# A residual seeded into the PSUM accumulators of a mixture-of-experts layer by identity products, with the final norm read from PSUM

## Chip, cores and metric

The kernel runs on one core of a Trainium2 chip. The metric is the device time of one execution in microseconds (us). Three executions of the kernel before took 1356.05, 1356.93 and 1356.97 us, median 1356.93. The profile and the trace come from a further execution of the same program.

Names used below: PE is TensorE (PEld its weight loads), DVE is VectorE, ACT is ScalarE, POOL is GpSimd, SP is SyncE, which issues most transfers.

## What is computed

One layer on 256 tokens of 1024 channels, all in float32: a mixer (causal pooling and a gated DeltaNet), then a top-4-of-32 mixture of experts, each with its residual, then a final RMSNorm. The part that matters here, cut from the reference:

```python
h = rmsnorm(x, norm_ffn_g[l]) * (1.0 + sc2) + sh2
x = x + gt2 * moe_ffn(h, router_w[l], router_b[l], exp_w1[l], exp_b1[l], exp_w2[l], exp_b2[l])
...
return rmsnorm(x, final_norm_g)

def rmsnorm(x, g):
    y = xf * lax.rsqrt(jnp.mean(xf * xf, axis=-1, keepdims=True) + RMS_EPS)
    return (y * g.astype(jnp.float32)).astype(x.dtype)
```

`moe_ffn` adds up, for each token, four experts' outputs with their gate weights, and each expert's bias `b2` with the same weight.

## The kernel before

The program is written by hand: each engine has its own list of instructions, in the order in which they stand, and the engines meet by semaphores. Nothing reorders the work.

**Weights.** All large weights pass through `ring`, six slots of 2 MB in SBUF. SP waits until a slot is free (`used[s]`, raised by the last product that reads it) and issues the next chunk into it (L504 in `stream`). An expert is six chunks: slots 0 to 3 hold w1, slots 4 and 5 the two halves of w2. SP issues them strictly in this order, so a slot that is late holds back those behind it. The chunks of expert 0 are loaded ahead; those of expert 1 onward wait for the routing (`vec_route`) and for block 0 to free the slots.

**Blocks.** The tokens of an expert are served in blocks of 64 (`SLOTS`). Blocks run in order of experts; here one expert has two blocks and each other one, 33 in all. Block 0 is written out, `serve` is the loop's body, `serve_last` the last block. For a block n PE does: `bias` (L1330), the w1 products (`hidden`, L1338), the gather of the next block's tokens (L1309), `combine` of block n - 1 (L1384), and `finish_block`: transposes (L1402, L1322, L1316) and the w2 products (L1372), which free slots 4 and 5 at their ends. In block 0, where there is no earlier block to combine, `biases_out` (L1396) stands in its place.

**Accumulators.** The layer's output for the 2 x 128 tokens and 2 x 512 channels is held in four PSUM banks, 4 to 7, over the whole expert loop. `biases_out` starts them with the gated b2 biases (`start=True`); each `combine` adds a block to them (`start=False`). The halves h = 0 and h = 1 of such a pair of products stand on different partitions of their operands (0 and 64), and so on different row groups of the array.

**Tail.** The last `combine` raises `pe_moe` after each half of the tokens. DVE adds the residual `xt` to each bank (`add_experts`, L1902) into `fin`; ACT squares the sums and accumulates the row sums (`fin_square`, L775); DVE turns one of each pair of sums into a half mean (L1906), ACT takes the root (L784), DVE its reciprocal (L1911), then scales by it and by the final gain (L1914). SP writes out each quarter (L520).

`ident` is a 128 x 128 identity matrix. `xt` lies in the tile `region_x` and has held the residual stream since the mixer's end; `fin` lies in `qkv`, `b2_rows` in `work`, `gatewT` in `region_z`.

Of the kernel before, what the change touches and what calls it, by code (L numbers as in the profile page):

```python
# [20 lines left out]
ALU = mybir.AluOpType  # L21
ACT = mybir.ActivationFunctionType
# [90 lines left out]
def program(nc, x, c, ada_w, ada_b, norm_mix_g, norm_ffn_g, w_in, conv_w, pool_w, pool_scale, a_log,  # L113
            dt_bias, gdn_norm_g, w_pool_out, w_gdn_out, w_out, router_w, router_b, exp_w1, exp_b1,
            exp_w2, exp_b2, final_norm_g, const, out):
    with ExitStack() as ctx:
        ctx.enter_context(nc.allow_non_contiguous_dma(reason="small parameter rows"))

        def sb(name, shape, dt=F32):
            return ctx.enter_context(nc.sbuf_tensor(name, shape, dt))  # L120

        def sem(name):
            return ctx.enter_context(nc.semaphore(name))
# [22 lines left out]
        small = sb("small", [P, 48])  # L146
        blocks_i = sb("blocks_i", [1, 2 * P + E + 1], I32)

        def const_tile(name):
            o, w = CONST[name]  # L150
            return consts[:, o:o + w]

        ident = const_tile("ident")
# [8 lines left out]
        xt = region_x[:, :].rearrange("p (t d) -> p t d", t=T)  # L162
# [51 lines left out]
        def take(n, parts=P):  # L214
            nonlocal m
            a = work[0:parts, m:m + n]
            m += n
            return a
# [17 lines left out]
        fin_g = take(D)  # L236
        fin = q_of.rearrange("p h s -> p (h s)").rearrange("p (t d) -> p t d", t=T)
        fin_sq = xn2
# [15 lines left out]
        bank = [ctx.enter_context(nc.psum_tensor(f"bank{i}", [P, 512], F32)) for i in range(8)]  # L254
# [18 lines left out]
        fin_in = sem("fin_in")  # L273
# [123 lines left out]
        pe_moe = sem("pe_moe")  # L397
# [8 lines left out]
        vec_b2 = sem("vec_b2")  # L406
        vec_blocks = sem("vec_blocks")
        act_fin = sem("act_fin")
        vec_fin = sem("vec_fin")
        vec_rms = sem("vec_rms")  # L410
        act_rms = sem("act_rms")
        vec_out = sem("vec_out")
# [24 lines left out]
        for n, (kind, _) in enumerate(chunks):  # L437
            chunk_no.setdefault(kind, []).append(n)
# [130 lines left out]
        def _(act):  # L569
# [201 lines left out]
            nc.scalar.activation(stat[:, 1, 2:3], small[:, 16:17], ACT.Sqrt)  # L771

            def fin_square(i):
                act.wait_ge(vec_fin, i + 1)
                nc.scalar.activation(fin_sq[:, i // 2, (i % 2) * 512:(i % 2 + 1) * 512],  # L775
                                     fin[:, i // 2, (i % 2) * 512:(i % 2 + 1) * 512], ACT.Square,
                                     accum_out=stat[:, 0, i:i + 1]).then_inc(act_fin, 1)

            for t in range(T):
                fin_square(2 * t)  # L780
                fin_square(2 * t + 1)
                act.wait_ge(act_fin, 2 * t + 2)
                act.wait_ge(vec_rms, t + 1)
                nc.scalar.activation(small[:, 20 + t:21 + t], stat[:, 0, 2 * t + 1:2 * t + 2], ACT.Sqrt, scale=1.0 / D,  # L784
                                     bias=small[:, 18 + t:19 + t]).then_inc(act_rms, 1)
# [3 lines left out]
        def _(pe):  # L789
# [141 lines left out]
            for r in range(2):  # L931
                for j in range(4):
# [3 lines left out]
                                          start=(r == 0), stop=(r == 1))  # L936
# [40 lines left out]
            for r in range(4):  # L977
                pe.wait_ge(pool_sq, 2 * r + 2)
                for j in range(4):
                    mm = nc.tensor.matmul(bank[4][32 * j:32 * j + 32, 0:S], pick[:, 31 - r:63 - r],  # L980
                                          sq[:, 2 * r + j // 2, (j % 2) * S:(j % 2 + 1) * S],
                                          start=(r == 0), stop=(r == 3))
# [17 lines left out]
            for r in range(4):  # L1000
                if r:
                    pe.wait_ge(vec_norm, 4 * r)
                for j in range(4):
# [3 lines left out]
                                          start=True, stop=True)  # L1007
# [47 lines left out]
            for g in range(2):  # L1055
                hs = [HG * g + h for h in range(HG)]
                lo, hi = slice(0, HALF), slice(HALF, P)
                for t in range(T):
# [8 lines left out]
                    for h in hs:  # L1067
                        nc.tensor.matmul(quad(3 * t + 1)[:, h % HG], k_of[:, h, tok], k_of[:, h, tok],
                                         start=True, stop=True)
                    for h in hs:  # L1070
                        mm = nc.tensor.matmul(quad(3 * t + 2)[:, h % HG], k_of[:, h, tok], q_of[:, h, tok],
                                              start=True, stop=True)
# [26 lines left out]
                else:  # L1099
                    for k in range(KC):  # L1100
                        mm = nc.tensor.matmul(bank[6][:, 0:E], mod[:, 24 + k:25 + k].to_broadcast([P, P]), rw[:, k, :],
                                              start=(k == 0), stop=(k == KC - 1))
                    mm.then_inc(pe_spread, 1)

                def turn_l(t):
                    for h in range(HG):
# [5 lines left out]
                                 start=True, stop=True).then_inc(pe_oct, 1)  # L1112
# [21 lines left out]
                for i, s in enumerate(LEVELS):  # L1134
                    z_tile(2 * g + 1, 1, 2 * i, 2 * i + 2)
                    for t in range(T):
                        pe.wait_ge(pool_off, 10 * g + 2 + 2 * i + (t + 1 if i else 2 - t))
                        pe.wait_ge(vec_inv, 10 * g + 2 * i + t + 1)
                        for h in range(HG):
                            if s < HALF:  # L1140
                                mm = nc.tensor.matmul(quad(3 * t + 1)[:, h], off[:, t, h], inv[:, t, h],  # L1141
                                                      start=True, stop=True)
                            else:
                                mm = nc.tensor.matmul(quad(3 * t + 1)[hi, h, lo], off[lo, t, h, hi], inv[lo, t, h, lo],
                                                      start=True, stop=True)
                        mm.then_inc(pe_prod, 1)
                    for t in range(T):
# [3 lines left out]
                        if s < HALF:  # L1151
# [4 lines left out]
                            for h in range(HG):  # L1156
                                mm = nc.tensor.matmul(quad(3 * t + 2)[:, h], prod[:, t, h], invT[:, t, h],  # L1157
                                                      start=True, stop=True)
                        else:
                            for h in range(HG):  # L1160
                                mm = nc.tensor.matmul(quad(3 * t + 2)[lo, h, hi], prod[hi, t, h, lo], invT[hi, t, h, hi],
                                                      start=True, stop=True)
                        mm.then_inc(pe_corr, 1)
                for t in range(T):
# [3 lines left out]
                    if t:  # L1168
                        for h in range(HG):
                            mm = nc.tensor.matmul(quad(3 * t + 1)[:, h], kbg[:, t, h], invT[:, t, h],  # L1170
                                                  start=True, stop=True)
# [17 lines left out]
                for h in range(HG):  # L1189
                    mm = nc.tensor.matmul(quad(3)[:, h], q_of[:, HG * g + h, P:2 * P], state[:, h],  # L1190
                                          start=True, stop=True)
# [100 lines left out]
            for t in range(T):  # L1292
                mm = nc.tensor.matmul(bank[5][:, t * E:(t + 1) * E], const_tile("before"), mask[:, t, :],
                                      start=True, stop=(t == 0))
# [94 lines left out]
            def biases_out():  # L1389

                pe.wait_ge(vec_route, 1)
                pe.wait_ge(vec_b2, 2)
                for t in range(T):
                    for h in range(2):
                        at = slice(h * SLOTS, h * SLOTS + E)
                        nc.tensor.matmul(bank[4 + 2 * t + h][:, :], gatewT[at, t * P:(t + 1) * P], b2_rows[at, :],  # L1396
                                         start=True, stop=False, skip_group_check=True)

            def turn_sel(n):
                pe.wait_ge(vec_wsel, n + 1)  # L1400
# [23 lines left out]
            def serve_last(n):  # L1424
# [21 lines left out]
                             start=True, stop=True).then_inc(pe_route, 1)  # L1446
# [15 lines left out]
            w1_chunk(0, 3)  # L1462
            gather(1)
            biases_out()
            finish_block(0)
            n_last = further_blocks(pe, serve)
# [5 lines left out]
        def _(dve):  # L1472
            chain = [0]

            def link(*steps):

                for ins in steps:
                    chain[0] += 1
                    ins.then_inc(vec_chain, 1)
                dve.wait_ge(vec_chain, chain[0])  # L1480

            tt, ts, stt = nc.vector.tensor_tensor, nc.vector.tensor_scalar, nc.vector.scalar_tensor_tensor
# [413 lines left out]
            serve(0)  # L1896
            serve(further_blocks(dve, serve), last=True)

            def add_experts(t, half):
                cut_ = slice(half * 512, (half + 1) * 512)  # L1900
                dve.wait_ge(pe_moe, t + 1)
                tt(fin[:, t, cut_], bank[4 + 2 * t + half][:, :], xt[:, t, cut_], ALU.add).then_inc(vec_fin, 1)  # L1902

            def half_of_squares(t):
                dve.wait_ge(act_fin, 2 * t + 1)
                ts(small[:, 18 + t:19 + t], stat[:, 0, 2 * t:2 * t + 1], 1.0 / D, EPS, ALU.mult, ALU.add)\  # L1906
                    .then_inc(vec_rms, 1)

            def scale_out(t):
                dve.wait_ge(act_rms, t + 1)  # L1910
                link(recip(small[:, 22 + t:23 + t], small[:, 20 + t:21 + t]))  # L1911
                for half in range(2):
                    cut_ = slice(half * 512, (half + 1) * 512)
                    stt(fin[:, t, cut_], fin[:, t, cut_], small[:, 22 + t:23 + t], fin_g[:, cut_],  # L1914
                        ALU.mult, ALU.mult).then_inc(vec_out, 1)

            add_experts(0, 0)
            add_experts(0, 1)
            half_of_squares(0)
            add_experts(1, 0)  # L1920
            add_experts(1, 1)
            half_of_squares(1)
            dve.wait_ge(fin_in, 16)
            scale_out(0)
            scale_out(1)


# [25 lines left out]
```

## Time and profile before

| | |
|---|---|
| median of three executions | 1356.93 us (1356.05 to 1356.97) |
| the profiled execution's own time | 1355.68 us |
| its span in the trace | 1353.3 us |
| PE busy | 1282.3 us, 95% |
| DVE, ACT, POOL busy | 391.3, 188.2, 48.3 us |
| mean TensorE clock granted | 0.997 of full speed |
| moved by DMA | 471.71 MB, mean 349 GB/s |

Busy shares are means over stages with different limits. The stages here are the mixer (up to about 390 us), block 0 of the experts, the expert loop, and a tail of some 10 us after the last product. In the loop the share of the DMA engines and that of PE are both close to full, so the waits have to be read, not the shares.

### The profile page before, as it was taken

How to read it: one execution, taken by the hardware profiler on the slowest of the kernel's cores; microseconds unless marked ns; L12 is line 12 of the kernel's file. 1: busy time of each engine (PE TensorE's matmuls, PEld its weight loads, DVE VectorE, ACT ScalarE, POOL GpSimd, SP SyncE). 2: the span in 40 equal slices, each digit the busy share in tenths (PEclk: the TensorE clock that was granted, in tenths of full speed). 3: DMA queues.
4: the chain of work that ended last, by engine and by line, in shares of the span. 5: the costliest groups of instructions: out<-in, count | busy, mean ns of one | idle time of the engine just before them, and what ended most of it. 6: DMA issues, size and time to landing. Idle time of an engine off the chain costs nothing.

```text
span 1353.3 us, 17457 instructions
## 1 busy us (share of the span) xinstructions
PE 1282.3 (95%) x6549; PEld 624.1 (46%) x6550; DVE 391.3 (29%) x982; ACT 188.2 (14%) x401; POOL 48.3 (4%) x48
## 2 busy tenths in 40 slices
PE   7999999999999999989999998999999999999997
PEld 5788878898653333223333322333333322333332
DVE  1599574732252211112111111211211111121112
ACT  1110223422120110001100000100010000011001
POOL 1020012220000000000000000000000000000000
PEclk9999999999999999999999999999999999999999
DMA  9998550008349999999999999699999999999996
GB/s 334 357 375 299 206 187 1 1 27 316 124 152 407 426 426 426 425 426 426 428 426 426 426 425 426 253 427 423 426 429 426 426 427 425 426 425 429 427 426 248
DMA packets 69079, 471.71 MB, mean 349 GB/s; under 512 B 4093, under 2 KB 4410, under 8 KB 36154
## 3 DMA queue, kind: packets, MB, share of 16 engines
q1 hardware_dynamic: 68224, 469.62, 84.5%
q10 hardware_dynamic: 538, 1.13, 0.3%
q0 software_dynamic: 288, 0.55, 0.2%
q8 instruction: 21, 0.34, 0.1%
q14 instruction: 8, 0.07, 0.0%
HBM read 470.23 MB, written 1.05 MB: 348 GB/s over the span
## 4 chain that ended last, share of the span: by engine, by line
PE 54%; DMA 42%; DVE 1%; SPq 1%; ACT 1%; issue 1%; DVEq 0%
DMA ring<-in_exp_w_dram 40%; PE bank L1338 18%; PE bank L806 12%; PE bank L1372 6%; PE bank L1235 2%; DMA ring<-in_ada_w_dram 2%; PE bank L1024 2%; PE bank L1384 2%; PE bank L1309 2%; PE bank L900 1%; PE bank L1330 1%; PE bank L1157 1%; PE bank L1141 1%; PE bank L1154 1%; SPq L487 1%
## 5 line engine op out<-in xcount | busy, mean ns | idle before, releaser
L1338 PE MATMUL bank<-ring,work 128*64 128x512 f32 x2112 | 470.6, 596 | 47.3 <-DMA ring<-in_exp_w_dram 47.3
L1338 PEld LDWEIGHTS bank<-ring,work 128*64 128x64 f32 x2112 | 144.6, 137 | 368.9 <-issue 272.2
L1372 PE MATMUL bank<-ring,work 128*64 128x512 f32 x1056 | 234.1, 595 | 0.9 <-ACT work L749 0.5
L1372 PEld LDWEIGHTS bank<-ring,work 128*64 128x64 f32 x1056 | 72.9, 137 | 137.9 <-issue 136.6
L756 ACT ACTIVATE work<-work 128x256 f32<-128x256 f32 x66 | 27.5, 416 | 765.1 <-DVE work L1863 765.1
L1863 DVE TENSOR_SCALAR work<-bank 128x256 f32<-128x256 f32 x66 | 27.6, 419 | 350.4 <-PE bank L1338 350.4
L806 PE MATMUL bank<-region_h,ring 128*128 128x256 f32 x576 | 126.6, 380 | 0.0
L806 PEld LDWEIGHTS bank<-region_h,ring 128*128 128x128 f32 x576 | 108.8, 190 | 14.4
L1893 DVE TENSOR_TENSOR work<-bank,work 128x512 f32<-128x512 f32 x33 | 22.8, 692 | 313.8 <-PE bank L1372 313.8
L1384 PE MATMUL bank<-work 64*128 64x512 f32 x264 | 65.6, 615 | 0.8 <-DVE work L1893 0.8
L1309 PE MATMUL bank<-qkv,work 128*64 128x512 f32 x264 | 62.3, 592 | 0.2 <-DVE work L1801 0.2
L1879 DVE TENSOR_SCALAR work<-consts,region_z 128x128 f32 (+1 forms) x66 | 19.9, 345 | 87.7 <-issue 87.7
L1870 DVE TENSOR_TENSOR work<-work 128x256 f32<-128x256 f32 x66 | 40.7, 617 | 12.3 <-DVE work L1866 12.3
L1384 PEld LDWEIGHTS bank<-work 64*128 64x128 f32 x264 | 22.7, 186 | 43.2 <-issue 41.5
L1309 PEld LDWEIGHTS bank<-qkv,work 128*64 128x64 f32 x264 | 19.0, 137 | 37.4 <-issue 37.4
L1330 PE MATMUL bank<-work 32*64 32x512 f32 x264 | 35.9, 612 | 0.3 <-issue 0.3
L1505 DVE SCALAR_TENSOR_TENSOR region_z<-ring,c_act,region_z 128x512 f32<-128x512 f32 x48 | 35.6, 809 | 0.0
L1538 DVE SCALAR_TENSOR_TENSOR qkv<-bank,conv_cols,qkv 128x255 f32<-128x255 f32 (+2 forms) x72 | 31.3, 477 | 1.3
L900 PE MATMUL bank<-region_h,ring 128*128 128x256 f32 x128 | 28.8, 382 | 1.3 <-DVE region_h L1523 1.3
L1024 PE MATMUL bank<-region_h,ring 128*128 128x256 f32 x128 | 29.6, 379 | 0.0
L806 PE MATMUL bank<-region_z,ring 128*128 128x256 f32 x128 | 27.9, 380 | 1.0 <-DVE region_z L1736 1.0
L1866 DVE SCALAR_TENSOR_TENSOR work<-work 128x256 f32<-128x256 f32 x66 | 28.0, 425 | 2.3
(304 smaller groups left out, 953.6 us busy)
## 6 DMA issues: line engine op xcount, KB each, us to landing
ring<-in_exp_w_dram SPq DMA_DIRECT2D x190, 2048.0 KB, 23.6
ring<-in_ada_w_dram SPq DMA_DIRECT2D x12, 2048.0 KB, 12.4
ring<-in_w_in_dram SPq DMA_DIRECT2D x11, 2048.0 KB, 12.8
ring<-in_w_in_dram SPq DMA_DIRECT2D x4, 1024.0 KB, 17.2
ring<-in_w_gdn_out_dram SPq DMA_DIRECT2D x2, 2048.0 KB, 11.7
ring<-in_w_out_dram SPq DMA_DIRECT2D x2, 2048.0 KB, 16.6
ring<-in_exp_w_dram SPq DMA_DIRECT2D x4, 1024.0 KB, 23.5
ring<-in_w_pool_out_dram SPq DMA_DIRECT2D x1, 2048.0 KB, 8.4
```

The lines of the kernel that those rows point to most:

```text
L806: mm = nc.tensor.matmul(out_ap, w(k) if w else w_slot(n, j, k), rhs[:, k, :], start=(k == 0), stop=(k == kc - 1))
L900: mm = nc.tensor.matmul(pair(i)[:, a, :], w_slot(n, 2 * (i % 2) + a, k), hT[:, k, :], start=(k + a == 0), stop=(k == KC - 1), skip_group_c ...
L1024: mm = nc.tensor.matmul(pair(7)[:, a, :], w_slot(n, j, k), hT[:, k, :], start=(k == 0), stop=(k == KC - 1))
L1309: mm = nc.tensor.matmul(bank[3][h * SLOTS:(h + 1) * SLOTS, :], sel[:, t, :], h2[:, t, h * 512:(h + 1) * 512], start=(t == 0), stop=(t == T ...
L1330: nc.tensor.matmul(bank[b][h * SLOTS:(h + 1) * SLOTS, :], onehot[b * SLOTS:b * SLOTS + E, :], b1_rows[b * SLOTS:b * SLOTS + E, h * 512:(h ...
L1338: mm = nc.tensor.matmul(bank[b][h * SLOTS:(h + 1) * SLOTS, :], xT[:, c % 4, c // 4, :], slot_as(q, 2)[:, i, lo:lo + 512], start=False, sto ...
L1372: mm = nc.tensor.matmul(bank[2][o * SLOTS:(o + 1) * SLOTS, :], actT[:, b, c, h, :], slot_as(4 + b, 2)[:, h, lo:lo + 512], start=(b + h + c ...
L1384: mm = nc.tensor.matmul(bank[4 + 2 * t + h][:, :], wselT[at, t * P:(t + 1) * P], y_nat[at, :], start=False, stop=last, skip_group_check=True)
L1505: ins = stt(half, w[:, k, :], c_act[:, k:k + 1], half, ALU.mult, ALU.add)
L1538: steps.append(stt(qkv[:, f, shift:S], src[:, a, 0:S - shift], w, qkv[:, f, shift:S], ALU.mult, ALU.add))
L1866: stt(lin[:, b, :], lin[:, b, :], 1.0, glu[:, b, :], ALU.add, ALU.mult).then_inc(vec_lin, 1)
L1870: tt(act_nat[:, b, :].rearrange("q (c p) -> q p c", c=2), lin[:, b, :].rearrange("q (p c) -> q p c", c=2), sig[:, b, :].rearrange("q (p c) ...
```

## The change

Each of the four accumulators is now started by an identity product of the residual (`ident` times `xt`, K = 128, 512 columns), and the bias product is added to it. `add_experts` and its semaphore `vec_fin` go. ACT's squares wait for the last `combine` and read the PSUM banks; DVE's scaling reads the banks too and writes `fin`. The scaling is split in single quarters, with the second half mean between the first two and the wait for the final gain (`fin_in`) ahead of the first reciprocal.

```diff
@@ scalar engine, fin_square
-                act.wait_ge(vec_fin, i + 1)
-                nc.scalar.activation(fin_sq[:, i // 2, (i % 2) * 512:(i % 2 + 1) * 512],
-                                     fin[:, i // 2, (i % 2) * 512:(i % 2 + 1) * 512], ACT.Square,
+                act.wait_ge(pe_moe, i // 2 + 1)
+                nc.scalar.activation(fin_sq[:, i // 2, (i % 2) * 512:(i % 2 + 1) * 512], bank[4 + i][:, :], ACT.Square,
                                      accum_out=stat[:, 0, i:i + 1]).then_inc(act_fin, 1)
@@ tensor engine, biases_out
+                        nc.tensor.matmul(bank[4 + 2 * t + h][:, :], ident, xt[:, t, h * 512:(h + 1) * 512],
+                                         start=True, stop=False, skip_group_check=True)
                         nc.tensor.matmul(bank[4 + 2 * t + h][:, :], gatewT[at, t * P:(t + 1) * P], b2_rows[at, :],
-                                         start=True, stop=False, skip_group_check=True)
+                                         start=False, stop=False, skip_group_check=True)
@@ vector engine, tail
-            def add_experts(t, half):
-                cut_ = slice(half * 512, (half + 1) * 512)
-                dve.wait_ge(pe_moe, t + 1)
-                tt(fin[:, t, cut_], bank[4 + 2 * t + half][:, :], xt[:, t, cut_], ALU.add).then_inc(vec_fin, 1)
...
-            def scale_out(t):
+            def invert(t):
                 dve.wait_ge(act_rms, t + 1)
                 link(recip(small[:, 22 + t:23 + t], small[:, 20 + t:21 + t]))
-                for half in range(2):
-                    cut_ = slice(half * 512, (half + 1) * 512)
-                    stt(fin[:, t, cut_], fin[:, t, cut_], small[:, 22 + t:23 + t], fin_g[:, cut_],
-                        ALU.mult, ALU.mult).then_inc(vec_out, 1)
-
-            add_experts(0, 0)
-            add_experts(0, 1)
+
+            def scale_out(t, half):
+                cut_ = slice(half * 512, (half + 1) * 512)
+                stt(fin[:, t, cut_], bank[4 + 2 * t + half][:, :], small[:, 22 + t:23 + t], fin_g[:, cut_],
+                    ALU.mult, ALU.mult).then_inc(vec_out, 1)
+
             half_of_squares(0)
-            add_experts(1, 0)
-            add_experts(1, 1)
+            dve.wait_ge(fin_in, 16)
+            invert(0)
+            scale_out(0, 0)
             half_of_squares(1)
-            dve.wait_ge(fin_in, 16)
-            scale_out(0)
-            scale_out(1)
+            scale_out(0, 1)
+            invert(1)
+            scale_out(1, 0)
+            scale_out(1, 1)
```

PE's order in block 0, from the gather for block 1 to the transposes of `finish_block`, before (`bankN` are PSUM banks; `work` and `region_z` hold `b2_rows` and `gatewT`):

```order
L1309 MATMUL bank3<-qkv,work 64x512 x4
L1396 MATMUL bank4<-work,region_z 128x512
L1396 MATMUL bank5<-work,region_z 128x512
L1396 MATMUL bank6<-work,region_z 128x512
L1396 MATMUL bank7<-work,region_z 128x512
L1402 MATMUL bank2<-consts,work 128x128 x2
```

And with the change (the lines above it move up by two, so L1307 is the gather that was L1309; `consts` holds `ident`, `region_x` holds `xt`):

```order
L1307 MATMUL bank3<-qkv,work 64x512 x4
L1394 MATMUL bank4<-region_x,consts 128x512
L1396 MATMUL bank4<-work,region_z 128x512
L1394 MATMUL bank5<-region_x,consts 128x512
L1396 MATMUL bank5<-work,region_z 128x512
L1394 MATMUL bank6<-region_x,consts 128x512
L1396 MATMUL bank6<-work,region_z 128x512
L1394 MATMUL bank7<-region_x,consts 128x512
L1396 MATMUL bank7<-work,region_z 128x512
L1402 MATMUL bank2<-consts,work 128x128 x2
```

An identity product now stands ahead of each bias product; the four bias products no longer follow one another.

DVE's order from the last block's scaling by `gt2` to its end, before:

```order
L1893 TENSOR_TENSOR work<-bank2,work 128x512
L1902 TENSOR_TENSOR qkv<-bank4,region_x 128x512
L1902 TENSOR_TENSOR qkv<-bank5,region_x 128x512
L1906 TENSOR_SCALAR small<-stat 128x1
L1902 TENSOR_TENSOR qkv<-bank6,region_x 128x512
L1902 TENSOR_TENSOR qkv<-bank7,region_x 128x512
L1906 TENSOR_SCALAR small<-stat 128x1
L1911 RECIPROCAL small<-small 128x1
L1914 SCALAR_TENSOR_TENSOR qkv<-qkv,small,work 128x512 x2
L1911 RECIPROCAL small<-small 128x1
L1914 SCALAR_TENSOR_TENSOR qkv<-qkv,small,work 128x512 x2
```

And with the change:

```order
L1893 TENSOR_TENSOR work<-bank2,work 128x512
L1901 TENSOR_SCALAR small<-stat 128x1
L1906 RECIPROCAL small<-small 128x1
L1910 SCALAR_TENSOR_TENSOR qkv<-bank4,small,work 128x512
L1901 TENSOR_SCALAR small<-stat 128x1
L1910 SCALAR_TENSOR_TENSOR qkv<-bank5,small,work 128x512
L1906 RECIPROCAL small<-small 128x1
L1910 SCALAR_TENSOR_TENSOR qkv<-bank6,small,work 128x512
L1910 SCALAR_TENSOR_TENSOR qkv<-bank7,small,work 128x512
```

The four adds are gone, the scalings read the banks, and the second half mean stands between the first two scalings instead of ahead of all four.

## Rows read from the trace of the kernel before

**Rows 1.** The page: PE's busy time, and GB/s in 40 slices of the span.
```profile
PE 1282.3 (95%) x6549; PEld 624.1 (46%) x6550; DVE 391.3 (29%) x982; ACT 188.2 (14%) x401; POOL 48.3 (4%) x48
...
GB/s 334 357 375 299 206 187 1 1 27 316 124 152 407 426 426 426 425 426 426 428 426 426 426 425 426 253 427 423 426 429 426 426 427 425 426 425 429 427 426 248
```

**Rows 2.** The chain that ended last, 420 to 500 us: start, length, what.
```profile
454.80 13.88 PE bank L1338 x64
...
481.60 13.88 PE bank L1338 x64
```

**Rows 3.** The same chain, 1000 to 1100 us.
```profile
1062.27 3.68 PE bank L1338 x16
...
1091.79 3.68 PE bank L1338 x16
```

**Rows 4.** The same chain, 800 to 960 us.
```profile
817.15 25.64 DMA ring<-in_exp_w_dram
...
842.83 3.65 PE bank L1338 x16
```

**Rows 5.** Windows: length, each engine's busy us, clock, DMA share, GB/s.
```profile
400.00:405.00 5.00, 5.00 (x28) 1.52 (x26) 1.46 (x9) 0.34 (x1) 0.00 (x0) 1.00 0.00 0
...
540.00:545.00 5.00, 4.46 (x24) 1.29 (x22) 0.00 (x0) 0.00 (x0) 0.00 (x0) 1.00 0.99 419
```

**Rows 6.** Two single issues into the ring, SP, tile view: duration ns, start, landing.
```profile
L504 SPq DMA_DIRECT2D ring<-in_exp_w_dram x1: 384/384/384, 423.7 to 423.7; - x1
...
DMA to landing us min/median/max: 10.8/10.8/10.8
...
L504 SPq DMA_DIRECT2D ring<-in_exp_w_dram x1: 342/342/342, 863.2 to 863.2; - x1
...
DMA to landing us min/median/max: 7.3/7.3/7.3
```

**Rows 7.** The chain that ended last, 380 to 560 us.
```profile
382.88 3.53 PE bank L1235 x8
...
415.09 1.72 PE bank L1309 x8
416.81 1.92 PE bank L1396 x8
418.73 0.37 PE bank L1402 x2
419.10 0.22 PE bank L1322 x2
```

**Rows 8.** Weight loads of L1235: duration ns min/median/max, first and last start.
```profile
L1235 PEld LDWEIGHTS bank<-ring,region_y x64: 188/190/192, 355.6 to 385.4; 128*128 128x128 f32 x64
```

**Rows 9.** Timeline of the tail: start, us, engine, line, what [idle before <- releaser].
```profile
1342.68 0.69 DVE L1893 TENSOR_TENSOR work<-bank,work 128x512 f32<-128x512 f32 x1 [7.69 <-PE bank L1372]
...
1344.61 1.29 DVE L1902 TENSOR_TENSOR qkv<-bank,region_x 128x512 f32<-128x512 f32 x2 [1.23 <-PE bank L1384]
1345.33 0.63 ACT L775 ACTIVATE qkv<-qkv 128x512 f32<-128x512 f32 x1 [4.89 <-DVE qkv L1902]
...
1346.70 0.29 ACT L784 ACTIVATE small<-stat,small 128x1 f32<-128x1 f32 x1
...
1347.63 0.15 DVE L1906 TENSOR_SCALAR small<-stat 128x1 f32<-128x1 f32 x1 [0.20 <-ACT qkv L775]
1347.71 0.16 DVE L1911 RECIPROCAL small<-small 128x1 f32<-128x1 f32 x1
1347.91 1.42 DVE L1914 SCALAR_TENSOR_TENSOR qkv<-qkv,small,work 128x512 f32<-128x512 f32 x2
...
1348.25 0.29 ACT L784 ACTIVATE small<-stat,small 128x1 f32<-128x1 f32 x1
...
1349.43 1.41 DVE L1914 SCALAR_TENSOR_TENSOR qkv<-qkv,small,work 128x512 f32<-128x512 f32 x2
```

**Rows 10.** A copy from PSUM by ACT, timeline of the routing.
```profile
397.10 0.60 ACT L741 ACTIVATE work<-bank 128x512 f32<-128x512 f32 x1 [3.59 <-PE bank L1309]
```

More of the change, by code:

```diff
@@ L408, in program @@
         act_fin = sem("act_fin")
-        vec_fin = sem("vec_fin")
         vec_rms = sem("vec_rms")
```

## The prediction

> **What bounds the kernel now.** I read the page first, then the chain of waits, then the weight transfers one by one, then the last 12 us. On the page TensorE is busy 95% of the span, yet the GB/s row stands at about 426 in nearly every slice from the twelfth on [rows 1]: two resources run close to each other, and which one sets the pace has to be read stretch by stretch. In the chain, early in the expert loop, nothing but TensorE appears and one expert takes 481.60 - 454.80 = 26.8 us [rows 2]. Later the same line starts again after each landing of a weight transfer, 1091.79 - 1062.27 = 29.5 us apart [rows 3]. Six chunks of 2 MB are an expert, so a chunk takes 29.5 / 6 = 4.92 us of DMA. TensorE needs 2.7 us less per expert than the DMA engines do; a lead or a lag of TensorE is used up, a lag of the transfers is kept. The one expert that has two blocks does not free it: TensorE waits for a landing at 842.79 just before it [rows 4], and the transfers that restart in its second block are set off by TensorE's own progress, so they inherit any lag.
>
> So what counts of the first block is when its slots are freed. The DMA engines are idle at 400 to 405 us [rows 5]: all six slots are full and the routing is being worked out. The stream starts at 406, fed by slots as block 0 frees them. The fifth chunk of the second expert is issued at 423.7, when the first half of the w2 product has ended, and lands 10.8 us later, at 434.5. A chunk that is issued to idle DMA engines lands after 7.3 us (the issue at 863.2) [rows 6]. The fifth chunk therefore has 10.8 - 7.3 = **3.5 us of slack**; past that, each microsecond TensorE loses before it frees this slot moves the whole stream.
>
> **Part 1: four identity products in the first block.** They stand between gather(1) and finish_block(0), ahead of both w2 products, so ahead of the release of the fifth slot. TensorE works without a gap there (the chain has only TensorE across that stretch), so all they add is added in full.
> - Identity product: K = 128, 128 columns of weights, 512 moving columns, float32. The same form is L1235: eight records, two for each product, in 3.53 us [rows 7], 0.88 us each. Four: 3.5 us.
> - The four bias products take 1.92 us today [rows 7] because the two halves stand on different row groups (partitions 0 and 64) and run side by side, two at a time: 4 steps, (1.92 - 0.2) / 4 = 0.43 us each. With a full-array product between any two of them they can't pair. Alone each takes its two passes, 0.86 us. Four: 3.4 us.
> - Change of array shape: eight of them where there was one. The four steps of L1396 take 1.92 us, eight steps of L1309 without a change take 1.72, so going into a row group costs 0.2 us; L1402's two transposes after it take 0.37, L1322's two 0.22, so going back costs 0.15 [rows 7]. Four each way: 1.4 us. Bounds: 0 us, if the next weight load hides under the running product; and 0.35 us each, 2.8 us, if a whole weight load (0.19 us [rows 8]) and the 0.15 both show. I take 1.4, since the rows nearest are the very changes in question.
>
> Together 3.5 + 3.4 + 1.4 = 8.3 us, say 8.4, in place of 1.92: TensorE is **6.5 us later** at finish_block(0) (bounds 5.0 and 7.8). The Trainium skill, page "TensorEngine Tiling (Array Packing)", section "Tiling Modes", says that changing the tiling mode drains TensorE, while changing only the tile doesn't. By that rule the 1.4 us belong in the sum; without a drain the sum below would be 1.4 us smaller, at +0.3. The trace agrees so far, with 0.15 to 0.2 us at the two changes.
>
> Slip of the stream: 6.5 - 3.5 = **3.0 us** (bounds 1.5 and 4.3). The chunks behind have more slack: the sixth is freed 3.5 us after the fifth (half of the w2 work), less than a chunk's 4.92, and TensorE gains 2.7 us per expert. The rest of TensorE's lag, 3.5 us, is gone within two experts, so its first wait for a landing comes one or two experts later than now (between 540 and 545 us [rows 5]). At the end only the 3.0 us stay. The Trainium skill, page "DMA: Bandwidth & Descriptors", section "Anatomy of one DMA", gives 2.0 us fixed plus bytes at 436 GB/s: as an estimate 6.8 us for a 2 MB chunk, so 4.0 us of slack and a sum 0.5 us lower. The trace has 7.3, and it decides.
>
> **Part 2: the tail.** Today VectorE adds the residual (two 512-column adds, 0.64 us apart), and only then ScalarE squares. Now ScalarE starts when TensorE has ended half 0 of the combine.
> - The first square moves from 1345.33 to 1344.61 [rows 9], 0.72 us earlier. ScalarE's row of work is as before: a 512-column read of PSUM takes 0.60 us [rows 10], the square from SBUF some 0.61. Its roots move from 1346.70 to 1345.98 and from 1348.25 to 1347.53, ending 1347.82.
> - VectorE loses four adds. It is no longer held by the second pair and the half mean behind it (1347.63) before it can scale. Reciprocal at 1346.31, first scaling 0.20 later (as 1347.71 to 1347.91) at 1346.51; 0.71 each. It reads PSUM now; L1893 does that in 0.69. Then the half mean (0.08), second scaling to 1348.01, reciprocal (0.10), two more scalings to 1349.53. Today they end at 1349.43 + 1.41 = 1350.84. **Gain 1.3 us.** The bound is now VectorE's four scalings; ScalarE's second root is in time by 0.2 us. The four output transfers keep following the scalings; the last one's 2 us to landing stay.
> - The dropped semaphore and the earlier wait for the final gain vector cost nothing: that vector is loaded ahead of the expert loop.
> - Bounds: 0 if the new reads of PSUM stretch ScalarE's row by 0.3 us per square; 1.4 if scalings take 0.69.
>
> **Sum.** 3.0 - 1.3 = **+1.7 us**. Against the profiled execution's own time of 1355.68 us this gives 1357.4. That execution lies 1.25 us below the median of the runs, 1356.93, so for a median I say 1358.6. A measurement of this kernel tells about 0.2% from no change, 2.7 us, so I forecast no difference that can be told.
>
> **Rivals.**
> 1. *The stream doesn't slip (12%).* If the products overlap better than the rows say, or the fifth chunk's transfer has other slack, the first block's loss is hidden and only the tail counts: -1.3 us, 1355.6. For: transfers bound the loop and TensorE has 2.7 us per expert to spare. Against: the slack is 3.5 us by two rows, and even without any cost of changing shape TensorE is 5.0 us late.
> 2. *Slower than can be overlooked (12%).* Every change between full array and row group shows a full weight load as well as a drain, 0.35 us. Then TensorE is 7.8 us late, the stream slips 4.3, the sum is +3.0: 1359.9. It decides from a lag of 7.5 us on, that is when the eight products take over 9.4 us, 1.18 us each. Against: the two changes of shape in the rows show 0.15 and 0.2 only; for: those stand behind a pair or behind short transposes, not behind a 512-column product.
> 3. *The tail gives nothing (6%).* ScalarE or VectorE reads of PSUM run slower while TensorE still writes the other two accumulators. Then +3.0 us, 1359.9, slower. Against: L1893 and the 0.60 us copies read PSUM beside a busy TensorE at full rate.
> 4. *Faster by over 0.2% (2%).* It would need more than the tail holds: the whole tail after the last combine is under 10 us and 1.3 of it go.
>
> **How the numbers follow.** Forecast 68%: a sum between +0.2 and +2.6, likeliest +1.7. With rival 1 inside the 0.2% as well, same is 0.80; rivals 2 and 3 give slower 0.17; faster 0.03. The range goes from rival 1 to rival 2, 1355.6 to 1359.9, with 0.2 and 0.7 us for the 0.9 us by which the three runs differ: 1355.4 to 1360.6.
>
> **What would show it.** In the trace of the changed kernel: L1394 and L1396 together 8.2 to 8.6 us from first start to the transposes of L1402, eight products without overlap; the fifth chunk of the second expert issued near 430.2 and landing near 437.5, with DMA engines idle for 2 to 3 us between 428 and 431; TensorE's first wait for a landing one or two experts later; the landing that now comes at 842.79 near 845.8; the first square right behind the first half of the last combine and the last scaling some 5.0 us after that square begins (now 6.2 from the first add). Wrong: a chunk that lands at 434.5 as before, or a block 0 longer by over 7.5 us.

## The result and the profile after

| | before | with the change |
|---|---|---|
| median, us | 1356.55 (1355.12 to 1359.87, 20 runs) | 1359.61 (1357.81 to 1361.64, 20 runs) |
| ratio | | 1.002, 95% interval 1.0013 to 1.0026 |
| profiled execution: span, us | 1353.3 | 1357.6 |

The change costs 3.1 us, some 0.2%: at the border of what I had called no difference, though the interval leaves out 1. The median lies in the range I gave (1355.4 to 1360.6), 1.0 us above the value I gave. Against the median of the kernel before, the likeliest sum was +1.7, and 3.1 were measured.

Not all 4.3 us between the two spans belong to the change. The mixer ahead of it, which it doesn't touch, varies from execution to execution: the first chunk that block 0 sets off is issued at 406.1 in the trace of before, at 407.4 here, and between 405.4 and 410.0 in all traces below. So I measure from that issue on. From it to the end of the span it is 1353.3 - 406.1 = 947.2 us before and 1357.6 - 407.4 = 950.2 with the change: **+3.0 us**, which is what the medians say.

The chain of waits in block 0 of the changed kernel, the answer to L1309, L1396 and L1402 in [rows 7] (start, length, what):

```profile
416.36 1.72 PE bank L1307 x8
418.07 1.06 PE bank L1394 x2
419.13 1.05 PE bank L1396 x2
420.18 1.05 PE bank L1394 x2
421.24 1.05 PE bank L1396 x2
...
424.39 1.06 PE bank L1394 x2
425.45 1.05 PE bank L1396 x2
426.50 0.37 PE bank L1402 x2
```

Eight products, each alone, 1.05 us each. From 418.07 to 426.50 it is 8.43 us where 1.92 stood: TensorE is 6.5 us late, as forecast. The full-array products (128 rows) take 1.05 us here, while L1235, the same form, takes 0.88 in a row of its like: the change of shape adds to the product instead of hiding under it.

What the DMA engines did meanwhile (windows of 5 us; the last column is GB/s):

```profile
425.00:430.00 5.00, 5.00 (x26) 2.27 (x26) 0.00 (x0) 1.53 (x4) 0.00 (x0) 1.00 0.72 306
430.00:435.00 5.00, 5.00 (x28) 1.51 (x28) 0.19 (x1) 0.00 (x0) 0.00 (x0) 1.00 0.52 136
```

In place of a steady 426 GB/s there is a hole: by the packets in the trace fewer than half of the 16 DMA engines work from 428.7 us on, and none between 430.1 and 432.5. The fifth chunk of the second expert is the next issue, the answer to the first of [rows 6]:

```profile
L503 SPq DMA_DIRECT2D ring<-in_exp_w_dram x1: 384/384/384, 431.5 to 431.5; - x1
...
DMA to landing us min/median/max: 7.6/7.6/7.6
```

It lands 7.6 us after its issue, as a chunk does that finds nothing ahead of it; before it took 10.8. Counted from the first issue it lands at 431.5 + 7.6 - 407.4 = 31.7 us, before at 28.4: the stream slips 3.3 us here.

The tail, the answer to [rows 9]:

```profile
1349.00 1.99 PE L1382 MATMUL bank<-work 64*128 64x512 f32 x8 [0.79 <-DVE work L1893]
1350.18 0.60 ACT L774 ACTIVATE qkv<-bank 128x512 f32<-128x512 f32 x1 [4.16 <-PE bank L1382]
...
1351.48 0.29 ACT L782 ACTIVATE small<-stat,small 128x1 f32<-128x1 f32 x1
...
1351.87 0.17 DVE L1906 RECIPROCAL small<-small 128x1 f32<-128x1 f32 x1 [0.82 <-ACT small L782]
1352.07 0.75 DVE L1910 SCALAR_TENSOR_TENSOR qkv<-bank,small,work 128x512 f32<-128x512 f32 x1
...
1352.80 0.74 DVE L1910 SCALAR_TENSOR_TENSOR qkv<-bank,small,work 128x512 f32<-128x512 f32 x1
...
1353.65 1.41 DVE L1910 SCALAR_TENSOR_TENSOR qkv<-bank,small,work 128x512 f32<-128x512 f32 x2
```

ScalarE starts 1.18 us after the combine's start, where VectorE's add stood before, and the last scaling ends 1355.06 - 1350.18 = 4.88 us behind that; it was 1350.84 - 1344.61 = 6.23. The tail gives the 1.3 us of the sum.

So the trace holds 3.3 of loss, 1.3 of gain and +3.0 in all. One more microsecond is lost somewhere after the fifth chunk. It is in a single landing. It is the tenth chunk of the stream, five behind the late one. Issue and time to landing of the ninth and the tenth, first in the changed kernel:

```profile
L503 SPq DMA_DIRECT2D ring<-in_exp_w_dram x1: 333/333/333, 446.4 to 446.4; - x1
...
DMA to landing us min/median/max: 12.4/12.4/12.4
...
L503 SPq DMA_DIRECT2D ring<-in_exp_w_dram x1: 333/333/333, 449.8 to 449.8; - x1
...
DMA to landing us min/median/max: 14.9/14.9/14.9
```

They land at 458.8 and 464.8, 6.0 us apart (the figures shown are rounded; here and in the table below I take intervals from unrounded times). The same two chunks in the kernel before:

```profile
L504 SPq DMA_DIRECT2D ring<-in_exp_w_dram x1: 333/333/333, 438.6 to 438.6; - x1
...
DMA to landing us min/median/max: 15.5/15.5/15.5
...
L504 SPq DMA_DIRECT2D ring<-in_exp_w_dram x1: 332/332/332, 442.1 to 442.1; - x1
...
DMA to landing us min/median/max: 17.0/17.0/17.0
```

454.1 and 459.0, 4.9 apart. In the changed kernel the DMA queues show something else there (the window of 458 to 460 us; packets, MB, share of 16 engines' time):

```profile
q1 hardware_dynamic: 66, 0.88, 105.3%
q8 instruction: 1, 0.02, 3.3%
```

One packet of the queue that loads instructions: 3.3% of 16 engines' 2 us is 1.06 us of one engine. The kernel before has one too, at 450 to 452 us, with no widened interval around it. Whether the step (so I call such a widened interval) belongs to the change was the open question.

### The profile page after: what moved, and what is told of

Same layout as the page of the kernel before. It is cut to its first block, busy times and chain, and to the rows that moved or that the text cites. A ratio compares the mean times of both kernels' runs of the same rounds, so it can differ in the third digit from the quotient of the medians.

```text
span 1357.6 us, 17469 instructions
## 1 busy us (share of the span) xinstructions
PE 1291.4 (95%) x6557; PEld 628.0 (46%) x6558; DVE 388.5 (29%) x978; ACT 188.1 (14%) x401; POOL 48.3 (4%) x48
## 3 DMA queue, kind: packets, MB, share of 16 engines
HBM read 470.23 MB, written 1.05 MB: 347 GB/s over the span
## 4 chain that ended last, share of the span: by engine, by line
PE 56%; DMA 40%; DVE 1%; SPq 1%; ACT 1%; issue 1%; DVEq 0%
DMA ring<-in_exp_w_dram 38%; PE bank L1336 19%; PE bank L804 12%; PE bank L1370 7%; PE bank L1233 2%; DMA ring<-in_ada_w_dram 2%; PE bank L1022 2%; PE bank L1382 2%; PE bank L1307 2%; PE bank L898 1%; PE bank L1328 1%; PE bank L1155 1%; PE bank L1139 1%; PE bank L1152 1%; SPq L486 1%
## 5 line engine op out<-in xcount | busy, mean ns | idle before, releaser
L1863 DVE TENSOR_SCALAR work<-bank 128x256 f32<-128x256 f32 x66 | 27.6, 418 | 348.2 <-PE bank L1336 348.2
L1307 PE MATMUL bank<-qkv,work 128*64 128x512 f32 x264 | 62.3, 592 | 0.2 <-DVE work L1801 0.2
L1307 PEld LDWEIGHTS bank<-qkv,work 128*64 128x64 f32 x264 | 19.0, 137 | 37.5 <-issue 37.5
L804 PE MATMUL bank<-region_z,ring 128*128 128x256 f32 x128 | 27.9, 380 | 1.0 <-DVE region_z L1736 1.0
```

The costliest lines, as they stand in the source:

```text
L804: mm = nc.tensor.matmul(out_ap, w(k) if w else w_slot(n, j, k), rhs[:, k, :], start=(k == 0), stop=(k == kc - 1))
L1307: mm = nc.tensor.matmul(bank[3][h * SLOTS:(h + 1) * SLOTS, :], sel[:, t, :], h2[:, t, h * 512:(h + 1) * 512], start=(t == 0), stop=(t == T ...
```

## The experiments

Three theories. **A**, that of the prediction: the stream slips by TensorE's lag less 3.5 us, and nothing else happens. **B**: a stream that ran dry loses more than that. **C**: the tail gives less in the time than in the trace. After the first four, B was made more exact as **D**: the extra loss is one step of about 1 us at a packet of the instruction queue, and only where the stream has run dry before (its mechanism stands in what was expected of 14 spare products).

For each kernel the table gives TensorE's lag when block 0 frees the fifth slot (for the two late kernels, then when it frees the next slot, that of the first chunk of the third expert), the landing of the fifth chunk of the second expert from the first issue, the interval that stands out behind it, the time from the first issue to TensorE's restart ahead of the expert with two blocks (842.83 - 406.1 = 436.7 before), and from the first issue to the end of the span. All are differences of starts, landings and spans in the traces, good to 0.1 us.

| kernel | lag | fifth lands | step later | to the restart | to the end | time against before (measured together) |
|---|---|---|---|---|---|---|
| before | 0 | 28.4 | none | 436.7 | 947.2 | |
| before, again | 0 | 28.2 | none | 436.5 | 946.9 | |
| the change | 6.5 | 31.7 | 6.0 | 441.1 | 950.2 | 1.002 (1.0013 to 1.0026) |
| the change, again | 6.5 | 31.6 | 6.0 | 441.1 | 950.1 | |
| identity products, old tail | 6.5 | 31.6 | 6.2 | 441.3 | 951.7 | 1.0029 (1.0018 to 1.0040) |
| new tail alone | 0 | 28.3 | none | 436.7 | 946.1 | 0.9987 (0.9978 to 0.9996) |
| grouped | 3.6 | 28.7 | 6.1 | 438.2 | 947.3 | 1.0001 (0.9992 to 1.0010) |
| grouped, late | -1.6, then 4.0 | 28.4 | none | 436.9 | 946.0 | 0.9984 (0.9975 to 0.9993) |
| alternating, late | -1.6, then 6.8 | 28.3 | 6.1 | 439.5 | 948.7 | 1.0001 (0.9992 to 1.0010) |
| 8 spare products | 1.8 | 28.3 | none | 436.8 | 947.2 | |
| 14 spare products | 3.2 | 30.8 | none | 439.2 | 949.6 | 1.0011 (1.0001 to 1.0020) |
| 14 spare, again | 3.2 | 31.0 | none | 439.4 | 950.2 | |
| 30 spare products | 6.7 | 31.9 | 6.0 | 441.2 | 951.9 | 1.0036 (1.0023 to 1.0049) |
| 60 spare products | 13.4 | 38.6 | 6.5 | 448.4 | 958.9 | 1.0086 (1.0073 to 1.0099) |

An interval without a step is 4.9 to 5.0 us (4.75 once, right behind the step of 6.5).

**Identity products with the old tail.** To `biases_out` of the kernel before:

```diff
+                        nc.tensor.matmul(bank[4 + 2 * t + h][:, :], ident, xt[:, t, h * 512:(h + 1) * 512],
+                                         start=True, stop=False, skip_group_check=True)
                         nc.tensor.matmul(bank[4 + 2 * t + h][:, :], gatewT[at, t * P:(t + 1) * P], b2_rows[at, :],
-                                         start=True, stop=False, skip_group_check=True)
+                                         start=False, stop=False, skip_group_check=True)
```

Expected: 

> The kernel before with the four identity products added in the first block and its old tail (so the residual is counted twice in the output). Theory A (the stream slips by TensorE's lag less 3.5 us of slack, nothing else): block 0 is 6.5 us longer, the transfers from the fifth chunk of the second expert on 3.0 us late, +3.0 us in time. Theory B (running dry costs the stream something beyond the slip): +4.0 to +4.6 us. If both were wrong and the loop hid the products: 0.

Measured: median 1360.58 against 1357.02, +3.6; in the trace +4.5 from the first issue to the end, of it 4.6 ahead of the restart. This is B's number in the trace; the times alone (+2.4 to +5.4) would leave A's +3.0 open. It is also the first half of the sum by itself: 3.3 at the fifth chunk and the step again.

**The new tail alone.** The changed kernel with

```diff
-                        nc.tensor.matmul(bank[4 + 2 * t + h][:, :], ident, xt[:, t, h * 512:(h + 1) * 512],
-                                         start=True, stop=False, skip_group_check=True)
                         nc.tensor.matmul(bank[4 + 2 * t + h][:, :], gatewT[at, t * P:(t + 1) * P], b2_rows[at, :],
-                                         start=False, stop=False, skip_group_check=True)
+                                         start=True, stop=False, skip_group_check=True)
```

Expected: 

> The changed kernel without the four identity products (the output lacks the residual of the experts' half). Theory A and B: first block and stream as before, the last scaling ends 1.3 us earlier behind the last combine, -1.3 us. Theory C (the tail's gain is smaller in the time than in the trace, which would explain that the change cost 3.1 and not 1.7): 0 to -0.3 us.

Measured: 1354.76 against 1357.02, ratio 0.9987, -1.8 us with an interval of -3.0 to -0.5; in the trace -1.1. The tail's gain is real and C falls: its 0 to -0.3 lies outside.

**Grouped.** The four identity products first, then the bias products in pairs:

```diff
                 for t in range(T):
                     for h in range(2):
-                        at = slice(h * SLOTS, h * SLOTS + E)
                         nc.tensor.matmul(bank[4 + 2 * t + h][:, :], ident, xt[:, t, h * 512:(h + 1) * 512],
                                          start=True, stop=False, skip_group_check=True)
+                for t in range(T):
+                    for h in range(2):
+                        at = slice(h * SLOTS, h * SLOTS + E)
                         nc.tensor.matmul(bank[4 + 2 * t + h][:, :], gatewT[at, t * P:(t + 1) * P], b2_rows[at, :],
                                          start=False, stop=False, skip_group_check=True)
```

Expected: 

> The changed kernel with the four identity products first and the four bias products behind them, in pairs again. Theory A: identity 3.5 us, biases 1.9, two changes of array shape in place of eight: block 0 is 3.7 us longer, the stream slips 0.2 us, the tail gives 1.3: -1.1 us against before. Theory B: the stream runs dry for a moment all the same, +0 to +0.5 us. If the pairing did not come back (products to one bank, one behind the other): about as the change, +1.7.

The chain of its block 0:

```profile
416.54 3.63 PE bank L1393 x8
420.17 1.92 PE bank L1398 x8
422.08 0.37 PE bank L1404 x2
```

The pairs are back: 5.55 us for the same eight products that take 8.43 in turns. The order of four lines is worth 2.9 us of TensorE's time. The fifth chunk lands 0.3 us late, A's number. Then comes a step to 6.1 us, and the kernel is no faster than before (median 1356.54 against 1357.02, ratio 1.0001): B's number.

**Grouped and late.** The same, and

```diff
-            biases_out()
             finish_block(0)
+            biases_out()
```

Expected: 

> As the grouped one, with all eight products behind the w2 products of block 0 instead of ahead of them. The fifth and sixth slot are then freed 1.9 us earlier than before; the next slot (first chunk of the third expert) is freed 3.7 us later than before and has 12.6 - 7.3 = 5.3 us of slack. Theories A and B: no slip, only the tail, -1.3 us. If TensorE's lag itself counted and not the slots: as the grouped one placed ahead.

Measured: 1354.56 against 1357.02, ratio 0.9984 with an interval of 0.9975 to 0.9993, to the end 946.0 against 947.2. The DMA engines never stop, there is no step, and the tail's gain is left whole. This is the version that beats both kernels: 2.5 us below before in the medians of the runs taken together, and 5.0 below the median of the change, which was timed in other runs. It does the same work on TensorE as the grouped one; only which slots wait for it differs. The slots of w2 are freed 1.6 us earlier than before, the next one 4.0 later.

**Spare products: the price of a lag by itself.** The kernel before with 14, 60, 30 and 8 products of the identity by itself, 0.22 us each, into a bank that is free there:

```diff
             biases_out()
+            keep_warm(14, 2)
             finish_block(0)
```

Expected of 14: 

> The kernel before with 14 spare 128x128 products of the identity (0.22 us each, 3.1 us) ahead of finish_block(0), nothing else. Theory A (slip = lag less 3.5 us): no slip, 0. Theory D (each of the 16 DMA engines has its own backlog; a fetch of instructions of 16 KB holds one of them back by about 1 us; a second fetch costs nothing as long as an earlier one has left another engine further behind, and costs in full once a dry moment has let that one catch up): the dry moment has only just begun at 3.1 us, slip 0 to 0.9 us.

Expected of 60: 

> As the kernel with 14 spare products, with 60 of them: 13.2 us. Theory A: slip 9.7 us, and +9.7 in time. Theory D: 9.7 at once at the fifth chunk of the second expert, and 1.0 to 1.3 more in one single later chunk, where the trace has the next packet of the instruction queue: +10.8. Theory B as I first put it (a dry stream costs in proportion): more than 12.

Expected of 30: 

> As the kernel with 14 spare products, with 30 of them: 6.6 us, the lag of the change without its identity products and without any change of array shape between products. Theory A: slip 3.1 us. Theory D: 3.1 us at the fifth chunk and 1.0 to 1.3 in one later one, +4.2. If the new products did something beyond taking TensorE's time (a slower read of an operand, a bank), this one would stay at less than the kernel with the identity products and the old tail (slip 4.5 us).

Expected of 8: 

> Eight spare products, 1.8 us, half of the slack. Theory A and D: the fifth chunk lands 28.4 us after the first issue as before, and the loop is as before, 436.7 us from the first issue to the wait ahead of the expert with two blocks. If any lag of TensorE in block 0 costs: 437.5 or more.

With 8 nothing moves: 28.3, 436.8, 947.2. With 60 the fifth chunk is 10.2 us late (A: 9.7), then one interval is 6.5 us and the restart 11.7 late, between the theories (D: 10.8; B in proportion: over 12). With 30 the change is matched without an identity product, without a change of shape between products and with the old tail: 3.5 us at the fifth chunk, one interval of 6.0, 4.5 at the restart, as with the identity products. So the products of the change cost the time that they take in this place; nothing else about them is needed. The packet of the instruction queue is in the widened interval again (440 to 442 us; the fifth lands at 439.3 and the next at 445.3):

```profile
q1 hardware_dynamic: 103, 0.84, 101.0%
q8 instruction: 1, 0.02, 3.0%
```

With 14 both theories missed: 2.4 us at once at the fifth chunk, where A had none and D at most 0.9. It is issued before the one ahead has landed, at 428.7 us against 431.0, and lands 10.0 us later:

```profile
L504 SPq DMA_DIRECT2D ring<-in_exp_w_dram x1: 383/383/383, 428.7 to 428.7; - x1
...
DMA to landing us min/median/max: 10.0/10.0/10.0
```

Half a microsecond of the DMA engines' time there shows that the stream did run nearly dry all the same, and at the same distance from the first issue in the kernel before that it didn't (first 14 spare, then before; the last column is GB/s):

```profile
429.20:429.70 0.50, 0.50 (x6) 0.21 (x4) 0.00 (x0) 0.00 (x0) 0.00 (x0) 1.00 0.16 66
...
427.40:427.90 0.50, 0.50 (x8) 0.00 (x0) 0.32 (x1) 0.00 (x0) 0.00 (x0) 1.00 1.08 459
```

**Alternating, late.** The changed kernel, not grouped, with

```diff
-            biases_out()
             finish_block(0)
+            biases_out()
```

Expected: 

> The changed kernel with its eight alternating products (8.4 us) moved as they are behind the w2 products of block 0. The slots of w2 are freed 1.9 us earlier than before, the next slot 6.5 us later, against 5.3 us of slack: slip 1.2 us. Theory A: 1.2 - 1.3 = -0.1 us. Theory D: a dry moment, so the next fetch of instructions adds 1.0 to 1.3: about +1.0. If only the place before the w2 products mattered: -1.3.

The first chunk of the third expert is issued to idle DMA engines at 438.3 and lands 7.2 us later, 39.7 from the first issue against 38.3: slip 1.4 (A: 1.2). Three chunks on there is a step to 6.1, and the restart is 2.8 us late. To the end +1.5 against before (A: -0.1, D: +1.0); in the medians -0.3, with 1.2 us either way.

**Again: the change, 14 spare products, before.**

Expected of the change: 

> The changed kernel once more, for its trace. Theory D: from the first chunk that block 0 sets off to TensorE's wait ahead of the expert with two blocks 441.1 us again (before 436.7), 3.3 us at the fifth chunk of the second expert and about 1.1 in one later chunk with an instruction packet. If the second step was chance in one execution: 440.0.

Expected of 14 spare: 

> The kernel with 14 spare products once more. If the 2.4 us slip of the first trace was that execution's alone (its time was 2 us above its median): the fifth chunk lands 28.1 to 28.7 us after the first issue, not 30.8. If a lag just under the slack always costs that much: 30.8 again.

Expected of before: 

> The kernel before once more. Theory D: a packet of the instruction queue near 422 us goes with a landing interval of 5.5 us in place of 4.9, the one near 450 us with none, and the loop takes 436.7 us. If the place of such steps is chance: another interval stands out.

The restart of the changed kernel, in the chain of the second trace (first issue at 410.0):

```profile
825.39 25.64 DMA ring<-in_exp_w_dram
851.08 3.65 PE bank L1336 x16
```

851.08 - 410.0 = 441.1, as the first time, with the step in the same interval. The kernel before again has none behind its packet at 450. The 14 spare products land the fifth chunk at 31.0 again: the miss repeats, so it isn't chance in one execution.

**What follows.** The step isn't chance: it comes in seven traces of kernels whose stream ran dry (the change twice, identity products, grouped, alternating late, 30 and 60 spare), each time with a packet of the instruction queue between the two landings or less than 1 us ahead of the first, and in none of the five whose stream never did (before twice, 8 spare, new tail alone, grouped late), though each of these has such a packet near the same place. The two with 14 spare products have no later step either, but have lost 2.4 us at once.

The traces also show why. The semaphore of each chunk is raised sixteen times, which I read as once by each of the 16 DMA engines; a chunk has landed at the sixteenth. The times of these sixteen, in us from the first issue:

| kernel | fifth chunk of the second expert | tenth chunk of the stream |
|---|---|---|
| before | thirteen 26.3 to 26.9, then 27.6, 27.8, 28.4 | twelve 50.9 to 51.4, then 52.2, 52.3, 52.9, 52.9 |
| the change | sixteen 31.1 to 31.7 | fifteen 55.7 to 56.3, then 57.4 |
| 8 spare | thirteen 26.5 to 26.8, then 27.3, 27.7, 28.3 | twelve 51.0 to 51.4, then 51.8, 52.2, 52.7, 52.8 |
| 14 spare | fifteen 27.9 to 28.4, then 30.8 | fourteen 52.4 to 52.9, then 54.1, 55.4 |

This is D's mechanism. In the kernel before, three engines are behind the others from the fourth chunk on, the last by 1.5 us, and stay behind; instruction packets stand just ahead of that, at 423.9 and 424.4 us. The packet at 450.3 sets a fourth engine back, only as far as the last, and costs nothing. In the changed kernel the dry moment has let all sixteen draw level; the packet at 458.5 sets one back, 1.1 us behind the slowest of the rest, and every chunk after it waits for that one. With 14 spare products the next packet, too, sets an engine back (54.1), but one is further behind already.

The table also corrects the slack. Most engines had not 3.5 us of it but 1.7: with 6.5 us of lag they are 4.8 late at the fifth chunk, with 3.2 us 1.5 late, with 1.8 us by 0.2 or less. The 3.5 us hold for the one engine that was last anyway. So the stream loses the lag less 1.7 us, plus what its new last engine is behind the others, less what the old one was. What stays open is why, in both traces with 14 spare products, one engine comes out of the short pause 2.5 us or more behind most of the others.

## Why the prediction held, and where it was off

- *What bounds the kernel.* Right. TensorE's lag is used up and the lag of the transfers is kept: 60 spare products cost 13.4 us of TensorE and 11.7 of the stream; at the restart some 440 us after the first issue it is all there, and in the median +10.5. With 8 spare products, 1.8 us, nothing was lost.
- *Part 1, the products.* Right: 8.43 us measured against 8.4, a lag of 6.5 against 6.5. With 3.5 and 3.4 us for the products, the eight changes of shape cost 8.43 - 3.5 - 3.4 = 1.5 us together against the 1.4 taken, so the lower bound (hidden) and the upper (0.35 each) both fall. The eight were counted a little wrong: the way out at L1402 took 0.37 us before as after and lies outside the 8.43, and in its place the first identity product pays for the change from the gather's 64 columns to 128. By luck the two errors cancel. The Trainium skill's rule (page "TensorEngine Tiling (Array Packing)", section "Tiling Modes") is that a change of mode drains TensorE. The trace agrees that each change costs time, some 0.19 us.
- *Slip of the stream.* This is the term of the sum that was mis-sized: "Slip of the stream: 6.5 - 3.5 = 3.0 us". It measured 4.4 at the restart. The step that failed is the slack, 10.8 - 7.3 = 3.5 us: it was read from the last of the sixteen DMA engines, while thirteen of them had 1.7. At the fifth chunk this hardly showed (3.3 us), since the dry moment let the late engines draw level; the other 1.1 came when the next instruction packet set one engine back again. I had worked out that "the chunks behind have more slack", which is so, and took from it that nothing more could be lost.
- *Idle DMA engines* were forecast "for 2 to 3 us between 428 and 431": all of them stood for 2.4 us, from 430.1 to 432.5, with a start 1.3 us later than before. The fifth chunk was to be issued near 430.2 and land near 437.5; less the 1.3 us it was 430.2 and 437.8.
- *TensorE's first wait* was to come one or two experts later. It did by one; of the same windows as [rows 5] the changed kernel shows a full TensorE at 540, and the first gap at 575:

```profile
540.00:545.00 5.00, 5.00 (x28) 1.41 (x26) 0.69 (x1) 0.00 (x0) 0.00 (x0) 1.00 1.00 426
...
575.00:580.00 5.00, 3.96 (x20) 1.20 (x18) 0.00 (x0) 0.00 (x0) 0.00 (x0) 1.00 1.01 429
```

- *The tail.* Right: 1.3 us, 6.23 to 4.88 from the first work on the accumulators to the last scaling, and the new tail alone gives -1.1 in its trace.
- *Rivals.* The first (no slip) fell: the stream slipped 4.4 us. The second would have needed over 9.4 us for the eight products, 8.43 were measured: its mechanism didn't come, but its time nearly did, from another source. The third is out: reads of PSUM take 0.58 to 0.60 us in ScalarE and 0.70 to 0.75 in VectorE. The estimate of 6.8 us for a chunk that finds no queue was worked out from the Trainium skill (page "DMA: Bandwidth & Descriptors", section "Anatomy of one DMA"), which gives its fit for transfers issued by GpSimd, not by SP as here. In these traces such landings took 7.1 us or more, 7.6 in the changed kernel, so the row was the better base, and still 0.3 short here.
- *The chances.* I gave 0.80 to within 0.2% and 0.17 to slower. The measured 1.002 is on that line, its interval, 1.0013 to 1.0026, on both sides. With the 0.3 and the 1.1 us that the slip lacked the sum would have been +3.1, and the two chances near even. (The chances of rivals 2 and 3 add up to 0.18, not 0.17.)

## What to carry to other kernels

A product added to an engine with time to spare costs nothing only if no transfer waits for what stands behind it. List the slots that are freed behind the place, take for each the time from issue to landing less that of a transfer without a queue, less also what the slowest DMA engine is behind the rest (3.5 us became 1.7 here), and put the work behind the slot with the least slack: grouping the eight products and moving them past two slots turned +3 us into -2. The products on different row groups ran side by side only while nothing of another shape stood between them (1.92 us for four, against 1.05 each), so group by shape; here that alone was worth 2.9 us for eight products.

## What the runs showed of the hardware

A weight stream that ran dry lost more than the gap. One later interval between landings was 6.0 to 6.5 us in place of 4.9, where the queue that loads instructions had its next packet, while the same kind of packet cost nothing in a stream that never stopped. The sixteen updates of a chunk's semaphore show the cause: such a packet set one DMA engine back, which counted only when no other was as far behind. So the slack of a transfer, read off its landing, was that of the slowest engine (3.5 us); most had 1.7. A lag of 1.8 us cost nothing, one of 3.2 us cost 2.4, and from 3.6 us on, ahead of the w2 products, the stream lost the lag less about 2.
